# Row chunks with the high and low activations as one 512-column operand, halves added by VectorE; matrix inverse started from the identity

## The chip, the cores and the metric

The program runs on one core of one Trainium2 chip. The metric is device time in microseconds (us), the median of several executions. TensorE multiplies, VectorE (DVE) and ScalarE (ACT) read its results from PSUM, GpSimd (POOL) works on SBUF alone, SyncE (SP) issues the weight loads. PSUM has eight banks, and a bank holds 512 float32 numbers per partition.

## The reference, cut to what matters

A sequence of 256 tokens of width 1024 goes through two blocks of layers. The parts around the change:

```
u = rmsnorm(h);  proj = u @ w_in                  # a_b a_c a_v z xbc dt g_a g_b
y_a = (a_b * causal_dwconv(a_c * a_v, conv_w)) @ w_out_a          # 3 taps
xbc = silu(causal_dwconv(xbc, conv_w) + conv_b)   # 3072 channels, 4 taps
y_b = mamba2(z, xbc, dt);  h = h + (sig(g_a)*y_a + sig(g_b)*y_b) @ w_mix_out
h = h + cross_attention(rmsnorm(h), rmsnorm(mem)) # q = u @ w_q, k, v = mem @ w_kv
...
proj = h @ gdn_w_in                               # second block: 2304 channels of qkv
qkv = silu(causal_depthwise_conv(qkv, conv_w))    # 4 taps
sol = triangular_solve(I + lower, rhs)            # 64 x 64, 6 heads x 4 chunks
```

Feed-forward layers stand between these parts. Everything is float32.

## The kernel before, in words

Every weight matrix arrives as a stream of 237 chunks, each of two pieces of 128 x 1024 numbers (474 pieces). SyncE loads a piece into one of eight slots as soon as the piece eight before it is done (`piece_done`). ScalarE copies it to `w_hi`, rounded (line 1352); GpSimd makes the rest, `w_lo` = raw - `w_hi` (line 440, counted by `split_done`). Activations are split likewise, into `u_hi` and `u_lo`. A product is the sum of high x high, high x low and low x high. ScalarE calls `after(q)` in its queue, which makes `w_hi` up to six pieces ahead of piece q.

The order of all work is written out by hand, one list for each engine. A chunk's kind says how it is multiplied. In a "pair", "proj" or "acc" stage the activations are stationary and the weights move, 512 columns at a time. In a "row" stage (`row_stage`, lines 507 to 509 for its matmuls) the weights are stationary, 128 x 128, and the 256 tokens move: for each of the eight k tiles and each of two output tiles `t`, three matmuls of 256 columns into half a bank. Row chunk r uses bank r % 4 of banks 0 to 3, and waits with `row_free` for the chunk four before it. There are row stages dt, ba, mq0, mq1, kv_k and q1, and seven that the change touches, with 43 chunks: short_cv (8), short_b (4), xbc (12), mem_k (4), xq (4), mem2k (2), qkv (9).

What follows a row chunk:
- short_cv: ScalarE copies the even chunk to `ctmp`; VectorE multiplies it with the odd one (line 2171) and applies three taps (2174, 2179). short_b: VectorE multiplies (2186), ScalarE makes `h_hi` (1535), VectorE `h_lo` (2188).
- xbc and qkv (`conv` on ScalarE, `taps` on VectorE): ScalarE writes the first tap (1550, twice a chunk), VectorE adds three taps for each of two tiles from the bank (2009, six instructions), the last of which frees the bank, ScalarE applies silu (1555, counted by `conv_act`). Between the chunks VectorE runs the steps of `row_chain`, the step sizes on few rows (2025 to 2048); two of its links, an exponential and a logarithm, are ScalarE's (1572, 1574 in xbc). In xbc VectorE also scales `x_dt` (2218) behind chunks 7 to 10, after four transposes in TensorE's queue. Behind xbc, TensorE does half a z pair and then waits for all twelve `conv_act` before the scores (887). In qkv ScalarE squares each chunk (1759) and TensorE sums the squares (977) behind chunks 5, 6 and 7; behind qkv come transposes (991) and the spreads gc, kb (985).
- mem_k, xq, mem2k: one copy to SBUF (1996). mem2v, a pair stage, follows mem2k; attention follows xq.

The inverse of the 12 x 2 unit triangular 64 x 64 blocks is built by doubling: `LEVELS` 2 to 64. VectorE masks `lt` to `iE` (2494), forms I - iE (2498), TensorE transposes iE (1086), VectorE forms the transposed start (2502). Each level is then a product of 48 small matmuls (1102), a mask `iQ` (2536), twice as many products (1122, 1125), and an update `iYX` (2551). Pieces of the gz stage (`gate`) and transposes (`extra`) stand between the levels in TensorE's queue, and the scores of the memory attention in the last two (1041, with VectorE's maxima, 2510). The last level ends in `fullY` (2549), from which the products v0 (1175) are made.

## Time and profile before

| | |
|---|---|
| median of 3 runs | 1541.56 us (1540.18 to 1541.83) |
| profiled execution, whole | 1541.43 us |
| its span, first to last instruction | 1539.6 us |
| TensorE busy | 1509.3 us, 98% |
| TensorE weight loads busy | 1307.5 us, 85% |
| VectorE busy | 605.1 us, 39% |
| ScalarE busy | 830.3 us, 54% |
| GpSimd busy | 1155.9 us, 75% |
| mean granted clock of TensorE | 0.994 |

A busy share is an average over the whole span. Matmul records overlap, since each is shown from its start to the end of its results, so the time that a matmul costs is read from start to start. "idle before" names how long an engine sat idle just before an instruction, and who released it.

### The profile page before, as it was taken

The page shows a single profiled execution, that of the slowest core. Times are in us where ns is not written, and L with a number is a line of the kernel's source. Part 1 is how long each engine was busy: PE and PEld are TensorE (multiplying, and loading weights), DVE is VectorE, ACT ScalarE, POOL GpSimd, SP SyncE. Part 2 cuts the span into 40 slices and gives each one's busy share as a digit, 9 for nine tenths or more (in the row PEclk, how much of TensorE's full clock was granted, in tenths as well). Part 3 has the DMA queues.
Part 4 walks back from the last instruction along what each step waited for, and adds up shares of the span by engine and source line. Part 5 has one row for each costly group of instructions (what it writes and reads, how often), then busy time and mean ns, then how long its engine had stood idle before and what let it go on. Part 6 is the DMA issues. An engine that isn't in the chain of part 4 may idle for free.

```text
span 1539.6 us, 22902 instructions
## 1 busy us (share of the span) xinstructions
PE 1509.3 (98%) x9276; PEld 1307.5 (85%) x9276; DVE 605.1 (39%) x1008; ACT 830.3 (54%) x1293; POOL 1155.9 (75%) x499
## 2 busy tenths in 40 slices
PE   9999999999999999999999999999999999999997
PEld 7888889999878898888888898888888888888886
DVE  3111016447786712331330498772113747311101
ACT  6444364375756536364554687155445476564443
POOL 8888978888758888578869796317888963388893
PEclk9999999999999999999999999999999999999999
DMA  6555555565644555265555563105555542355552
GB/s 232 191 189 192 181 191 180 175 212 181 211 152 141 199 181 193 91 209 187 186 184 194 171 211 124 44 29 196 178 186 200 194 160 75 106 176 184 191 196 78
DMA packets 71865, 259.87 MB, mean 169 GB/s; under 512 B 7984, under 2 KB 8784, under 8 KB 71504
## 3 DMA queue, kind: packets, MB, share of 16 engines
q1 hardware_dynamic: 69552, 250.97, 49.4%
q10 hardware_dynamic: 2208, 7.43, 1.3%
q8 instruction: 74, 1.21, 0.3%
q14 instruction: 31, 0.25, 0.0%
HBM read 257.29 MB, written 1.08 MB: 168 GB/s over the span
## 4 chain that ended last, share of the span: by engine, by line
PE 83%; DVE 9%; ACT 4%; issue 2%; POOL 1%; DMA 1%; ACTq 0%; DVEq 0%; POOLq 0%
PE bank L537 14%; PE bank L539 14%; PE bank L538 13%; PE bank L567 5%; PE bank L569 5%; PE bank L568 5%; PE bank L507 5%; PE bank L509 5%; PE bank L508 5%; PE bank L681 1%; ACT w_hi L1352 1%; DVE dec L2231 1%; DVE dec L2234 1%; PE bank L653 1%; DVE sq_mem L2059 1%
## 5 line engine op out<-in xcount | busy, mean ns | idle before, releaser
L440 POOL TENSOR_TENSOR w_lo<-raw,w_hi 128x1024 fp32r<-128x1024 f32 x468 | 1129.0, 2445 | 337.6 <-ACT w_hi L1352 337.1
L1352 ACT ACTIVATE w_hi<-raw 128x1024 fp32r<-128x1024 f32 x474 | 487.9, 1058 | 286.1 <-DMA raw<-in_w 281.8
L537 PE MATMUL bank<-w_hi,u_hi 128*128 128x512 f32 x872 | 345.8, 397 | 2.4 <-POOL w_lo L464 2.0
L539 PE MATMUL bank<-w_hi,u_lo 128*128 128x512 f32 x872 | 340.9, 391 | 0.0
L538 PE MATMUL bank<-w_lo,u_hi 128*128 128x512 f32 x872 | 340.3, 390 | 0.0
L507 PE MATMUL bank<-u_hi,w_hi 128*128 128x256 f32 x688 | 196.7, 286 | 0.0
L537 PEld LDWEIGHTS bank<-w_hi,u_hi 128*128 128x128 f32 x872 | 164.3, 188 | 36.5 <-POOL w_lo L464 2.2
L509 PE MATMUL bank<-u_hi,w_lo 128*128 128x256 f32 x688 | 194.7, 283 | 0.0
L508 PE MATMUL bank<-u_lo,w_hi 128*128 128x256 f32 x688 | 194.6, 283 | 0.0
L539 PEld LDWEIGHTS bank<-w_hi,u_lo 128*128 128x128 f32 x872 | 164.0, 188 | 35.0
L538 PEld LDWEIGHTS bank<-w_lo,u_hi 128*128 128x128 f32 x872 | 164.4, 188 | 32.6
L567 PE MATMUL bank<-w_hi,h_hi 128*128 128x512 f32 x416 | 162.9, 392 | 0.0
L569 PE MATMUL bank<-w_hi,h_lo 128*128 128x512 f32 x416 | 162.0, 389 | 0.0
L568 PE MATMUL bank<-w_lo,h_hi 128*128 128x512 f32 x416 | 161.9, 389 | 0.0
L507 PEld LDWEIGHTS bank<-u_hi,w_hi 128*128 128x128 f32 x688 | 131.9, 192 | 1.6 <-issue 1.2
L508 PEld LDWEIGHTS bank<-u_lo,w_hi 128*128 128x128 f32 x688 | 132.0, 192 | 0.3
L509 PEld LDWEIGHTS bank<-u_hi,w_lo 128*128 128x128 f32 x688 | 132.0, 192 | 0.0
L1972 DVE TENSOR_TENSOR h_lo<-bank,h_hi 128x512 fp32r<-128x512 f32 x44 | 30.4, 691 | 227.9 <-ACT h_hi L1406 227.9
L1420 ACT ACTIVATE act_g<-bank,stats 128x256 f32<-128x256 f32 x88 | 41.7, 475 | 136.2 <-PE bank L539 136.1
L1985 DVE SCALAR_TENSOR_TENSOR hid<-bank,stats,act_g 128x256 f32<-128x256 f32 x88 | 42.4, 483 | 174.5 <-ACT act_g L1420 174.4
L1966 DVE SCALAR_TENSOR_TENSOR x<-bank,x 128x512 f32<-128x512 f32 x32 | 21.8, 688 | 197.2 <-PE bank L569 153.6
L569 PEld LDWEIGHTS bank<-w_hi,h_lo 128*128 128x128 f32 x416 | 78.1, 188 | 16.4
(432 smaller groups left out, 2072.0 us busy)
## 6 DMA issues: line engine op xcount, KB each, us to landing
raw<-in_w SPq DMA_DIRECT2D x474, 512.0 KB, 4.4
bc<-acs_scratch ACTq DMA_DIRECT2D x8, 512.0 KB, 4.6
mem_t<-in_mem ACTq DMA_DIRECT2D x2, 1024.0 KB, 6.3
xf<-in_x SPq DMA_DIRECT2D x2, 512.0 KB, 7.0
out<-out_t SPq DMA_DIRECT2D x4, 256.0 KB, 2.7
lvl<-in_lvl ACTq DMA_DIRECT2D x1, 448.0 KB, 3.0
band<-in_band ACTq DMA_DIRECT2D x1, 256.0 KB, 6.1
tri<-in_tri SPq DMA_DIRECT2D x1, 192.0 KB, 8.0
```

Source lines behind the costliest of these rows:

```text
L440: nc.gpsimd.tensor_tensor(w_lo[:, q % RAW, :], raw[:, q % RAW, :], w_hi[:, q % HI, :].bitcast(F32), ALU.subtract).then_inc(split_done, 1)
L507: mm(b[:, t, :], w1, hi[:, kt, :], start=first, stop=False, skip_group_check=True)
L508: mm(b[:, t, :], w1, lo[:, kt, :], start=False, stop=False, skip_group_check=True)
L509: m = mm(b[:, t, :], w0, hi[:, kt, :], start=False, stop=last, skip_group_check=True)
L537: mm(b[:], hi[:, kt, a], w_hi[:, q % HI:q % HI + 2, c], start=kt == 0, stop=False, skip_group_check=True)
L538: mm(b[:], hi[:, kt, a], w_lo[:, q % RAW:q % RAW + 2, c], start=False, stop=False, skip_group_check=True)
L539: m = mm(b[:], lo[:, kt, a], w_hi[:, q % HI:q % HI + 2, c], start=False, stop=kt == KT - 1, skip_group_check=True)
L567: mm(b, h_hi[:, q, a], w_hi[:, hsl, c], start=q == 0, stop=False)
L568: mm(b, h_hi[:, q, a], w_lo[:, rsl, c], start=False, stop=False)
L569: return mm(b, h_lo[:, q, a], w_hi[:, hsl, c], start=False, stop=q == n - 1)
L1352: fn(w_hi[:, q % HI, :], raw[:, q % RAW, :], ACT.Copy).then_inc(hi_made, 1)
L1985: v.scalar_tensor_tensor(out=hid[j % 2][:, s, :], in0=bank[FB[(2 * j + s) % 3]][:, 1, :], scalar=stat_of(norm, "rstd")[:, s:s + 1], in1=ac ...
```

## The change

The tiles of the high and low activations are interleaved (`u_both`, `mm_both`, `um_both`), so that high and low of one k tile are 512 neighbouring columns. In the seven stages `wide_stage` takes the place of `row_stage`: per k tile and output tile one matmul of 512 columns (`w_hi` against both) into a bank of its own, and one of 256 (`w_lo` against high) into its first half. A chunk then holds two of the four banks, 2r % 4 and the next. VectorE adds the two halves of each bank (`summed`, two reductions over the pair of numbers), which frees the chunk's banks (`row_free`). In mem_k, xq and mem2k the sum is written where the copy went. In short_cv, short_b, xbc and qkv it is written to one more bank (`sum_bank`), from which taps and products read; a new count `row_done` tells ScalarE, and the next sum, that its readers are through. ScalarE's copy to `ctmp` goes. Every row and pair stage waits for the last user of its bank (`freed_for`), and the second gc spread waits for the last taps of qkv, whose sum bank it uses. In the inverse, `iE`, its transposes and the first two updates go; a level 1 is added that takes the identity as its start, and the scores and maxima of memory heads 2 and 3 move behind the last level.

```diff
-LEVELS = [2, 4, 8, 16, 32, 64]
+LEVELS = [1, 2, 4, 8, 16, 32, 64]
-         ("bacols", 1), ("gc", 3), ("lcols", 1), ("kb", 3), ("masks", 1), ("la", 6), ("x0", 3)]
+         ("bacols", 1), ("gc", 3), ("lcols", 1), ("kb", 3), ("masks", 1), ("la", 6)]
...
+WIDE = ('short_cv', 'short_b', 'xbc', 'mem_k', 'xq', 'mem2k', 'qkv')
+STAGE_OF = [name for name, n, kind in ORDER if kind not in ("acc", "proj") for _ in range(n)]
...
+def banks_of(r):
+
+    name, j = STAGE_OF[r], r - G0[STAGE_OF[r]]
+    if name in WIDE:
+        return [2 * r % 4, 2 * r % 4 + 1]
+    if name.startswith("ffn"):
+        return [2 - j % 3]
+    if name in ("mq1", "q1") and r < G0["q1"] + 3:
+        return [(G0["mq1"] + (r - G0["mq1"]) % 2) % 4]
+    return [4] if (name, j) == ("gz", 2) else [r % 4]
+
+
+def freed_for(r, b):
+
+    return max([e + 1 for e in range(r) if b in banks_of(e)], default=0)
+
+
+DONE0 = {"short_b": 0, "xbc": 4, "qkv": 16}
...
-        u_hi = place("u_hi", [P, KT, S], F32R, 72)
-        u_lo = place("u_lo", [P, KT, S], F32R, 80)
+        u_both = place("u_both", [P, KT, 2, S], F32R, 72)
+        u_hi, u_lo = u_both[:, :, 0, :], u_both[:, :, 1, :]
...
+
+        def tile_bank(r, t):
+
+            return bank[banks_of(r)[t]]
+
+        def sum_bank(stage):
+
...
+
+        def memory_bank(i):
+
+            return bank[(3, 4, 3, 0)[i]]
...
+            def wide_stage(name, both, ready=None, sub=None):
+
+                j0, n = sub or (0, NUM[name])
+                for j in range(j0, j0 + n):
+                    r = G0[name] + j
+                    for h in range(2):
+                        q = P0[name] + 2 * j + h
+                        pe.wait_ge(split_done, q + 1)
+                        for t in range(2):
+                            b = tile_bank(r, t)
+                            if h == 0 and freed_for(r, banks_of(r)[t]):
+                                pe.wait_ge(row_free, freed_for(r, banks_of(r)[t]))
+                            for k in range(4):
+                                if ready and j == j0 and t == 0:
+                                    ready(4 * h + k)
+                                a, kt = slice(k * S + t * P, k * S + t * P + P), 4 * h + k
+                                mm(b[:], w_hi[:, q % HI, a], both[:, kt, :, :], start=kt == 0, stop=False, skip_group_check=True)
+                                m = mm(b[:, 0, :], w_lo[:, q % RAW, a], both[:, kt, 0, :], start=False, stop=kt == KT - 1, skip_group_check=True)
+                        m.then_inc(piece_done, 1)
-                        if h == 0 and r > 3:
-                            pe.wait_ge(row_free, r - 3)
+                        if h == 0 and freed_for(r, r % 4):
+                            pe.wait_ge(row_free, freed_for(r, r % 4))
...
-            row_stage("short_cv", u_hi, u_lo)
-            row_stage("short_b", u_hi, u_lo)
+            wide_stage("short_cv", u_both)
+            wide_stage("short_b", u_both)
...
-                row_stage("xbc", u_hi, u_lo, sub=(j, 1))
+                wide_stage("xbc", u_both, sub=(j, 1))
...
             spread("gc", 0, grow[6])
+            pe.wait_ge(W["row_done"], DONE0["qkv"] + NUM["qkv"])
             spread("gc", 1, grow[6])
...
-            for n in range(3):
-                if n == 1:
-                    gate(1, 1)
-                b = start_unit(U0["x0"] + n)
-                pe.wait_ge(W["lev_e"], 4 if n else 2)
-                for s in range(4):
-                    for p0 in (0, 64):
-                        a = slice(p0, p0 + 64)
-                        m = mm(b[a, 0, 64 * s:64 * s + 64], iE[a, 4 * n + s, :], ident[a, a], start=True, stop=True)
-                m.then_inc(unit_done, 1)
-            pe.wait_ge(row_free, G0["gz"] + 2)
...
-                    pe.wait_ge(unit_free, U0[f"inv{lev}"] + n - 2)
+                    pe.wait_ge(unit_free, U0[f"inv{lev}"] + n - 2 if li else U0["inv1"])
...
-                                m = mm(b[a, 0, o], lt[a, k % 6, c:c + 64], iX[a, k, :], start=True, stop=True)
+                                m = mm(b[a, 0, o], lt[a, k % 6, c:c + 64], iX[a, k, :] if li else ident[a, a], start=True, stop=True)
                     m.then_inc(unit_done, 1)
+                if li == 0:
+                    gate(1, 1)
+                if lev == 2:
+                    pe.wait_ge(row_free, G0["gz"] + 2)
                 for e in EXTRA_AT.get(lev, []):
                     extra(*e)
-                if li >= 4:
-                    memory_scores(2 * li - 8)
-                    memory_scores(2 * li - 7)
-                if li == 0:
-                    pe.wait_ge(W["lev_x"], 1)
+                if lev == 32:
+                    memory_scores(0)
+                    memory_scores(1)
...
-                                mm(b[a, 1, o], iY[a, k, :], iQ[a, k, :], start=True, stop=True)
+                                mm(b[a, 1, o], iY[a, k, :] if li else ident[a, a], iQ[a, k, :], start=True, stop=True)
                             for p0 in (0, 64):
                                 a = slice(p0, p0 + 64)
-                                m = mm(b[a, 0, o], iQ[a, k, :], iY[a, k, :], start=True, stop=True)
+                                m = mm(b[a, 0, o], iQ[a, k, :], iY[a, k, :] if li else ident[a, a], start=True, stop=True)
                     m.then_inc(W["s_step"], 1)
+            memory_scores(2)
+            memory_scores(3)
...
-                act.wait_ge(piece_done, a + 2)
-                if j >= 2:
-                    act.wait_ge(row_free, g - 2)
-                fn(ctmp[j % 2][:], bank[g % 4][:], ACT.Copy).then_inc(W["short_act"], 1)
...
-                    act.wait_ge(piece_done, done(stage, j + 1))
+                    act.wait_ge(row_free, G0[stage] + j + 1)
...
-                        m = fn(dst[:, i, :], bank[g % 4][:, t, :], ACT.Identity, scale=col(wname, k * i + k - 1), **kw)
+                        m = fn(dst[:, i, :], sum_bank(stage)[:, t, :], ACT.Identity, scale=col(wname, k * i + k - 1), **kw)
...
-                    act.wait_ge(row_free, G0[stage] + j + 1)
+                    act.wait_ge(W["row_done"], DONE0[stage] + j + 1)
...
+            def summed(stage, j, out):
+
+                for t in range(2):
+                    m = v.tensor_reduce(out[:, t, :], tile_bank(G0[stage] + j, t)[:].rearrange("p a c -> p c a"), AX.X, ALU.add)
+                m.then_inc(row_free, 1)
+
+            def sum_rows(stage, dst, j0=0, n=None):
+
+                for j in range(j0, n if n is not None else NUM[stage]):
+                    dve.wait_ge(piece_done, done(stage, j + 1))
+                    summed(stage, j, dst(j))
+
...
+                    dve.wait_ge(piece_done, done(stage, j + 1))
+                    if j:
+                        dve.wait_ge(W["row_done"], DONE0[stage] + j)
+                    summed(stage, j, sum_bank(stage))
                     dve.wait_ge(W["conv_first"], (0 if stage == "xbc" else 12) + j + 1)
-                    b = bank[(G0[stage] + j) % 4]
+                    b = sum_bank(stage)
                     for d in range(1, k):
                             if d == k - 1 and t == 1:
-                                m.then_inc(row_free, 1)
+                                m.then_inc(W["row_done"], 1)
...
+                dve.wait_ge(piece_done, P0["short_cv"] + 4 * j + 2)
+                summed("short_cv", 2 * j, ctmp[j % 2])
                 dve.wait_ge(piece_done, P0["short_cv"] + 4 * j + 4)
+                summed("short_cv", 2 * j + 1, sum_bank("short_cv"))
+                dve.wait_ge(row_free, g + 2)
+                v.tensor_tensor(cv[:, 2 * j:2 * j + 2, :], ctmp[j % 2][:], sum_bank("short_cv")[:], ALU.mult).then_inc(W["short_act"], 1)
                 dve.wait_ge(W["short_act"], j + 1)
-                v.tensor_tensor(cv[:, 2 * j:2 * j + 2, :], ctmp[j % 2][:], bank[(g + 1) % 4][:], ALU.mult).then_inc(row_free, 2)
-                dve.wait_ge(row_free, g + 2)
...
-                v.tensor_tensor(cc[:, a, :], cc[:, a, :], bank[(G0["short_b"] + j) % 4][:], ALU.mult).then_inc(row_free, 1)
+                summed("short_b", j, sum_bank("short_b"))
+                dve.wait_ge(row_free, G0["short_b"] + j + 1)
+                v.tensor_tensor(cc[:, a, :], cc[:, a, :], sum_bank("short_b")[:], ALU.mult).then_inc(W["row_done"], 1)
...
-            copy_rows("mem_k", lambda j: k_t[:, 2 * j:2 * j + 2, :], 0, 1)
+            sum_rows("mem_k", lambda j: k_t[:, 2 * j:2 * j + 2, :], 0, 1)
             merged_lo(2)
             merged_lo(3)
-            copy_rows("mem_k", lambda j: k_t[:, 2 * j:2 * j + 2, :], 1)
+            sum_rows("mem_k", lambda j: k_t[:, 2 * j:2 * j + 2, :], 1)
...
-            copy_rows("xq", lambda j: q_t[:, 2 * j:2 * j + 2, :])
+            sum_rows("xq", lambda j: q_t[:, 2 * j:2 * j + 2, :])
...
-            copy_rows("mem2k", lambda j: mk[j][:])
+            sum_rows("mem2k", lambda j: mk[j][:])
...
-            for c in range(2):
-                for p0 in (0, 64):
-                    a = slice(p0, p0 + 64)
-                    v.tensor_tensor(iE[a, 6 * c:6 * c + 6, :], lt[a, :, 256 * c + p0:256 * c + p0 + 64],
-                                    lvl[a, 0:1, a].to_broadcast([64, 6, 64]), ALU.mult).then_inc(W["lev_e"], 1)
-            dve.wait_ge(W["lev_e"], 4)
-            dve.wait_ge(W["eye_set"], 1)
-            v.tensor_tensor(iY, eye[:].unsqueeze(1).to_broadcast([P, GS, 64]), iE[:], ALU.subtract).then_inc(W["lev_x"], 1)
-            for n in range(3):
-                u = U0["x0"] + n
-                dve.wait_ge(unit_done, u + 1)
-                v.tensor_tensor(iX[:, 4 * n:4 * n + 4, :], eye[:].unsqueeze(1).to_broadcast([P, 4, 64]),
-                                bank_of(u)[:, 0, :].rearrange("p (k c) -> p k c", c=64), ALU.subtract).then_inc(unit_free, 1)
-            v.memset(fullY[64:P, :, 0:64], 0.0).then_inc(W["full_zero"], 1)
-
...
+                if li == 0:
+                    v.memset(fullY[64:P, :, 0:64], 0.0).then_inc(W["full_zero"], 1)
+                    dve.wait_ge(W["eye_set"], 1)
...
-                if li >= 4:
-                    memory_max(2 * li - 8)
-                    memory_max(2 * li - 7)
+                if lev == 32:
+                    memory_max(0)
+                    memory_max(1)
...
                     else:
-                        v.tensor_tensor(iYX[:, :, a, :], iYX[:, :, a, :], b, ALU.subtract).then_inc(unit_free, 1)
+                        now = iYX[:, :, a, :] if li else eye[:].unsqueeze(1).unsqueeze(1).to_broadcast([P, 2, 4, 64])
+                        v.tensor_tensor(iYX[:, :, a, :], now, b, ALU.subtract).then_inc(unit_free, 1)
+            memory_max(2)
+            memory_max(3)
```

## Rows read from the trace of the kernel before

**Rows 1.** The page, part 1: busy time, share of the span, instructions, by engine.
```profile
PE 1509.3 (98%) x9276; PEld 1307.5 (85%) x9276; DVE 605.1 (39%) x1008; ACT 830.3 (54%) x1293; POOL 1155.9 (75%) x499
```

**Rows 2.** Timeline of TensorE in short_cv: start, length, instruction.
```profile
240.11 0.28 PE L507 MATMUL bank<-u_hi,w_hi 128*128 128x256 f32 x1
...
241.55 0.28 PE L507 MATMUL bank<-u_hi,w_hi 128*128 128x256 f32 x1
```

**Rows 3.** Timeline of TensorE in mem2v, a pair stage.
```profile
870.53 0.39 PE L538 MATMUL bank<-w_lo,um_hi 128*128 128x512 f32 x1
...
875.54 0.39 PE L539 MATMUL bank<-w_hi,um_lo 128*128 128x512 f32 x1
```

**Rows 4.** Groups by form, VectorE: busy, mean ns of one, idle before.
```profile
L2091 DVE TENSOR_REDUCE small<-bank 128x2 f32<-128x512 f32 x4 | 2.8, 691 | 3.3 <-PE bank L735 3.1
```

**Rows 5.** Busy time in stretches: PE, PEld, DVE, ACT, POOL; granted clock; DMA.
```profile
319.00:393.00 74.00, 73.45 (x613) 73.08 (x612) 48.52 (x88) 48.50 (x67) 61.38 (x26) 1.00 0.60 199
...
886.00:942.00 56.00, 54.84 (x453) 52.55 (x453) 52.50 (x74) 45.64 (x62) 49.49 (x21) 1.00 0.56 187
...
977.00:1013.00 36.00, 34.99 (x822) 33.15 (x821) 25.12 (x57) 10.74 (x33) 0.00 (x0) 0.93 0.01 4
```

**Rows 6.** Timeline of VectorE, dt and xbc.
```profile
318.61 0.47 DVE L2198 TENSOR_SCALAR rows<-bank,par 32x256 f32<-32x256 f32 x1 [2.19 <-PE bank L509]
...
347.51 2.40 DVE L2035 TENSOR_TENSOR rows<-rows,rows 32x256 f32<-32x256 f32 x1
...
352.50 2.51 DVE L2039 TENSOR_TENSOR rows<-rows,rows 32x256 f32<-32x256 f32 x1
...
373.55 2.69 DVE L2009 SCALAR_TENSOR_TENSOR xbc<-bank,par,xbc 128x255 f32<-128x255 f32 x6 [2.68 <-ACT xbc L1550]
```

**Rows 7.** Timeline of ScalarE, xbc.
```profile
333.11 1.28 ACT L1572 ACT_TABLE_LOAD   x1
334.41 0.42 ACT L1572 ACTIVATE rows<-rows 32x256 f32<-32x256 f32 x1
...
336.62 0.99 ACT L1550 ACTIVATE xbc<-bank,par 128x256 f32<-128x256 f32 x2
```

**Rows 8.** Timeline of TensorE, end of the first z half.
```profile
397.63 0.59 PE L887 MATMUL bank<-xbc 128*128 128x256 f32 x2
```

**Rows 9.** Timeline of VectorE from mem2k to qkv.
```profile
872.18 1.27 DVE L1996 COPY mk<-bank 128x512 f32<-128x512 f32 x2
...
886.66 0.42 DVE L2400 COPY grow<-bank 6x256 f32<-6x256 f32 x1
...
889.60 4.74 DVE L2411 COPY pick<-ident 6x768 f32<-6x768 f32 x2
...
915.35 0.40 DVE L2035 TENSOR_TENSOR grow<-grow,grow 6x256 f32<-6x256 f32 x1
```

**Rows 10.** Timeline of TensorE, the first two gc spreads behind qkv.
```profile
942.47 2.00 PE L985 MATMUL bank<-grow,pick 128*128 128x256 f32 x8
```

**Rows 11.** Timeline of VectorE, short_cv.
```profile
240.94 8.00 DVE L2179 SCALAR_TENSOR_TENSOR cc<-cv,par,cc 128x255 f32<-128x255 f32 x4
...
253.81 1.79 DVE L2179 SCALAR_TENSOR_TENSOR cc<-cv,par,cc 128x255 f32<-128x255 f32 x4
```

**Rows 12.** Timeline of VectorE, last copy of xq.
```profile
629.11 0.69 DVE L1996 COPY q_t<-bank 128x512 f32<-128x512 f32 x1 [5.06 <-PE bank L509]
```

**Rows 13.** Timeline of VectorE, the inverse and its end.
```profile
964.01 9.31 DVE L2494 TENSOR_TENSOR iE<-lt,lvl 64x384 f32<-64x384 f32 x4
...
1010.33 0.69 DVE L2510 TENSOR_REDUCE small<-bank 128x2 f32<-128x512 f32 x1 [1.83 <-PE bank L1041]
```

**Rows 14.** Timeline of TensorE, the inverse.
```profile
968.24 0.68 PE L1086 MATMUL bank<-ident,iE 64*64 64x64 f32 x16
...
976.82 2.83 PE L1102 MATMUL bank<-iYX,lt 64*64 64x64 f32 x48 [2.20 <-DVE iYX L2502]
...
985.68 1.64 PE L1102 MATMUL bank<-iYX,lt 64*64 64x64 f32 x48
```

60 lines of the change are left out of this document (29 added, 31 removed).

## The prediction

> **What bounds the kernel now.** I read the page's busy shares first, then the waits and the timelines of the seven converted stages. TensorE is busy 98% of the span [rows 1], so only two things can shorten the run: fewer or shorter TensorE starts, or the 30 us in which it is idle (1539.6 - 1509.3). Every other engine costs nothing so long as it stays hidden. In the two convolution stages that cover is thin. Over xbc VectorE is busy 48.5 of 74 us, and over qkv 52.5 of 56 us; the granted clock is full in both [rows 5]. So VectorE in qkv has 3.5 us to spare, and the change gives it 18 more instructions there. That is the pair of numbers to keep in mind.
>
> **TensorE's saving.** A unit of a row stage (one k tile, one output tile) is three matmuls of 256 columns. From the first to the last row there are 12 starts in 1.44 us, 0.120 us each [rows 2], so 0.360 us a unit. The unit becomes one matmul of 512 columns and one of 256. In a pair stage 22 starts of 512 columns take 5.01 us, 0.228 us each [rows 3]. So a unit becomes 0.228 + 0.120 = 0.348 us, a chunk of 16 units 5.57 instead of 5.76 us: 0.19 us a chunk, 8.2 us over 43 chunks if nothing else stirred. The columns are the same 768; only one start's overhead of some 13 ns goes. Bounds of the unit: 0.360 (no gain) and 0.320 (768 columns at 2.4 GHz, no overhead at all; 27 us over all chunks). I take 0.348, which both rows give directly. The Trainium skill (TensorE: Matmul & The Clock Gate, Back-to-back issue gap) gives N/2.4 + 2.5 ns as the gap between starts; by that rule one start less would save 2.5 ns a unit, 1.7 us in all, an estimate from that page. The rows show 13 ns a start, and the measurement decides.
>
> **VectorE's new work.** Each chunk gets two reductions, each reading 512 numbers from PSUM. A reduction of 512 elements from PSUM takes 0.69 us [rows 4]; two back to back overlap a little, as the two copies that took 1.27 us [rows 9]. I take 1.3 us a chunk. That row reads neighbours and writes two numbers, whereas here the two summands lie 1 KB apart and 256 numbers are written, which no row shows. Upper bound 2.4 us a pair (the 512-element operations blocked by GpSimd are the nearest slow ones), lower bound 0.6 us (one pass over 512). The Trainium skill (VectorE: DVE Perf Modes, Rules for kernel authors) speaks against this part of the change: it calls the reduction the slowest VectorE operation, fixed at single rate, and advises restructuring where it is on a hot path.
>
> The order matters more than the length. Before, ScalarE's first tap of chunk j ran beside VectorE's taps of chunk j-1, and four banks let TensorE run up to four chunks ahead. Now the sum of chunk j waits for the taps of j-1 (one shared sum bank), ScalarE's first tap waits for the sum, VectorE's taps wait for ScalarE, and a chunk holds two banks, so TensorE can start chunk j only when the sum of j-2 is done. A turn of VectorE is then 1.3 (sums) + 1.0 (ScalarE, VectorE idle) [rows 7] + 2.7 (six taps) [rows 6] + 0.1 of handshakes = 5.1 us, before the small row steps between the chunks; TensorE needs 5.57.
>
> **xbc, walked.** Origin is the end of dt (318.6, where VectorE's bias row starts [rows 6]). Row steps by the trace: three steps after chunk 3 take 7.4 us (first and last of three [rows 6]), about 2.3 us after chunk 0, 0.3 after chunk 1, 3.6 after chunk 2, 1.8 after chunk 4; the steps of chunks 1 and 2 wait for a table load and an exponential or logarithm [rows 7]. x_dt adds 1.3 after chunks 7 to 10.
>
> | chunk | TensorE starts | sum done | taps done | VectorE free |
> |---|---|---|---|---|
> | 0 | 0.0 | 6.9 | 10.6 | 13.0 |
> | 2 | 11.1 | 20.5 | 24.6 | 29.2 |
> | 3 | 16.7 | 30.5 | 34.2 | 41.6 |
> | 4 | 22.3 | 42.9 | 46.7 | 48.4 |
> | 5 | 30.5 (2.7 late) | 49.7 | 53.5 | 53.5 |
> | 6 | 43.0 (6.9 late) | 54.8 | 58.5 | 58.8 |
> | 7 | 49.7 (1.0 late) | 60.1 | 63.8 | 65.1 |
> | 11 | 75.5 | 85.4 | 89.1 | 89.1 |
>
> TensorE is through xbc and the first z half at 88.1, but behind it waits for all twelve silus, at 89.8. The same walk of the kernel before gives 79.0, and the trace has 397.63 - 318.6 = 79.0 [rows 8]: the walk holds. Cost +10.8 us. With the pair at 2.4 us the walk gives 102.6 (+23.6), with 0.6 us 83.1 (+4.1). VectorE enters the decay chain 12 us later and TensorE the z pieces 10.8 us later, so at most 1.2 us could be added there; I take none. The load queue is no part of it: SyncE issues each raw piece when a piece is done, so it waits along with TensorE, and the DMA engines are 60% busy [rows 5]; ScalarE's and GpSimd's splits run ahead of TensorE and run dry instead of late. ScalarE also loses its four copies of short_cv, which saves nothing. The first xbc chunk also needs dt's bank back (0.47 us [rows 6]): +0.5.
>
> **qkv, walked the same way.** ba's bank is needed by chunk 0 (free at 887.1 [rows 9]), and VectorE is busy with the pick copies until 894.3 [rows 9]. Sums are done at 895.6, 902.8, 908.9, 919.7, 930.0, 938.7, 947.4, 952.2 and 961.1. TensorE is held 4.8 us before chunk 5, then 6.8, 3.8 and 1.7 us by the square sums, which wait for ScalarE's squares, which in its queue now stand behind a first tap that waits for a sum. Taps end at 964.6. (The same walk of before has TensorE through qkv at 942.2; the trace starts the gc spreads, behind two short transposes, at 942.47 [rows 10].) The second gc spread uses the sum bank and waits for the last taps; it stood in the middle of the row that starts at 942.47 [rows 10], at 943.3. Cost +21.3 us, +30 with the pair at 2.4, +16.5 at 0.6.
>
> **Other borders.** short_out needs the bank of the last short_b sum: +1.35. short_cv's first chunk needs gate_a's last sigmoid: +0.65. xq's first needs mem_v's last copy, +0.7, and attention waits for a pair of reductions in place of one copy of 0.69 [rows 12]: +0.6. mem2v, which started at 870.2, needs mem2k's sum, which VectorE reaches at 872.2 [rows 9], so 873.5: +3.3. In short_cv one set of four taps took 8.0 us where the others took 1.8 [rows 11]; with two banks a chunk such a set holds TensorE up to 4 us: I take 2, between 0 and 4. The 20 chunks outside xbc, qkv and mem2k save 3.8.
>
> **The inverse.** Gone are the masking of 9.3 us [rows 13] and the 3 us behind it. But gate pieces lay beside them: the last wait for VectorE there is 2.2 us [rows 14]. Now: the products of level 1 behind gate(1,0) at 968.3 [rows 14], 1.6 us as the 48 rows at 985.68 [rows 14], gate(1,1) 2.9, the second products (twice as many, same pace) 3.0: level 2 at 975.8 instead of 976.8, and its first part takes 1.6 instead of 2.8 us [rows 14]: -2.2. At the end, two maxima no longer stand before fullY [rows 13]: -1.8. Sum -4.
>
> **Sum.** -3.8 + 10.8 + 0.5 + 21.3 + 6.6 + 2.0 - 4.0 = +33.4 us. Against it stands a relief: while TensorE stalls GpSimd runs dry, and then row steps are short. One and the same step took 2.40 us in xbc and 0.40 in qkv [rows 6, 9], with GpSimd busy 83% and 88% of the two stretches [rows 5]. The walk has some 24 us of such excess; GpSimd's share falls by a tenth in xbc and by a quarter in qkv, worth about 4 us. The result is +29.5 on the profiled execution's 1541.4 us (span 1539.6 and 1.8 around it, 0.1 below the median of the runs): **1571 us**.
>
> **The rivals.**
> *All of it hidden (faster).* If the row steps took 0.4 us throughout and a pair 0.6 us, the walks give -3.0 in xbc and +3 in qkv; with borders of 5.0 (short_cv's stall gone), the inverse at -4 and the saving of 3.8, that is -2.8; a unit of 0.320 would take up to 19 more off: 1520 to 1539. It decides only if VectorE's pair falls below about 0.6 us and GpSimd stops blocking. For it: the stalls themselves relieve GpSimd. Against: six taps and ScalarE's first tap alone fill 3.7 us of each turn. Chance 0.07, and 0.05 for no change.
> *Relief larger than taken.* Row steps of 0.4 us with a pair of 1.3 us: +1.6 and +7.5, in all about +8.5: 1550. Chance 0.10.
> *Reductions at half rate for the 1 KB stride.* +23.6, +30, borders 4 more: +60, 1601 us. Nothing in the trace bears on it. Chance 0.12.
> *The clock.* Where TensorE waits in the inverse the granted clock is 0.93 over 36 us [rows 5], 2.5 us lost. Stalls of 7 us may do the same in xbc and qkv: +2 to +5, inside the forecast.
> *The forecast* (1558 to 1590) has 0.66.
>
> **Range and chances.** 1552 to 1600 leaves out the faster and equal cases, the lowest relief and the worst of the half rate. 0.2% (3 us) is about what a measurement here can tell. Faster 0.07, same 0.05, slower 0.88.
>
> **What would show it.** Starts of 0.228 and 0.120 us in turn; reductions near 0.69 us, one ending before each first tap; TensorE waiting for VectorE's sums in xbc (3, 7 us) and qkv, and for squares there; a wait before the second gc spread; level 2 of the inverse at most 1 us earlier relative to the last lt. The forecast is wrong if VectorE's row steps shorten to 0.4 us throughout, or if the reductions are not near 0.69 us.

## The result, and the profile after

The changed kernel takes 1582.44 us (median of 4 runs, 1580.27 to 1583.85), the kernel before 1541.43 (1540.18 to 1541.83): a ratio of 1.0269, 95% interval 1.0257 to 1.0281, 41.0 us slower. The page of the profiled execution (span 1582.0 us) answers to [rows 1]:

```profile
PE 1520.5 (96%) x8688; PEld 1280.6 (81%) x8688; DVE 629.8 (40%) x1082; ACT 829.4 (52%) x1289; POOL 1156.9 (73%) x499
```

TensorE is idle for 61.5 us (1582.0 - 1520.5) where it was idle for 30.3. VectorE has 24.7 us more to do on balance: the reductions take 55 us, while copies, the masking of the inverse and waits for GpSimd inside other instructions are gone. That is little for an engine busy 40% of the span; what it costs depends on where it stands. The view of waits of TensorE names the places (waiting line, releaser, us in total, times, longest):

```profile
PE bank L561 <- DVE bank L2038: 11.1, 4, 4.8
PE bank L561 <- DVE ctmp L2038: 8.2, 2, 7.2
PE bank L1030 <- ACT l2sq L1802: 5.3, 1, 5.3
PE bank L1038 <- DVE qkv L2068: 4.9, 1, 4.9
...
PE bank L590 <- DVE mk L2038: 3.1, 1, 3.1
...
PE bank L880 <- DVE x_dt L2282: 2.0, 1, 2.0
```

L561 is the first matmul of `wide_stage` and L2038 the reduction: 19.3 us of waits for sums. L1030 are the square sums, L1038 the gc spreads, L880 the transposes behind xbc chunks. Following one start of TensorE through both timelines gives the loss by stage. "Later by" is how much later than before the named work starts:

| start of | before, us | after, us | later by | added by the stage ahead of it |
|---|---|---|---|---|
| short_cv | 224.64 | 224.88 | 0.2 | 0.2 |
| short_out | 293.75 | 304.73 | 11.0 | 10.7 |
| dt | 315.54 | 326.59 | 11.1 | 0.1 |
| scores behind xbc | 397.63 | 421.40 | 23.8 | 12.7 |
| mem2k | 857.22 | 880.56 | 23.3 | -0.4 |
| ba, behind mem2v | 882.70 | 910.39 | 27.7 | 4.4 |
| kb products, behind qkv and the spreads | 958.47 | 1005.35 | 46.9 | 19.2 |
| v products, behind the inverse | 1017.10 | 1059.33 | 42.2 | -4.6 |

The reductions are what the prediction took them for. The groups by form of VectorE answer to [rows 4]; 58 of them take 0.685 us each, and a pair stands in the timelines as 1.28 to 1.30 us:

```profile
L2038 DVE TENSOR_REDUCE bank<-bank 128x256 f32<-128x512 f32 x58 | 37.2, 685 | 26.0 <-PE bank L562 25.9
...
L2038 DVE TENSOR_REDUCE k_t<-bank 128x256 f32<-128x512 f32 x8 | 5.2, 686 | 16.7 <-PE bank L562 16.7
```

**short_cv.** VectorE's timeline answers to [rows 11]. The two scalings and four taps of the first pair took 5.0 + 10.0 us, and the sums that give banks back stand behind them:

```profile
238.42 5.01 DVE L2236 TENSOR_SCALAR cc<-cv,par 128x256 f32<-128x256 f32 x2
243.47 10.00 DVE L2241 SCALAR_TENSOR_TENSOR cc<-cv,par,cc 128x255 f32<-128x255 f32 x4
253.40 1.28 DVE L2038 TENSOR_REDUCE ctmp<-bank 128x256 f32<-128x512 f32 x2
```

In the kernel before, the two scalings ahead of the set of 8.0 us took 3.7:

```profile
237.24 3.67 DVE L2174 TENSOR_SCALAR cc<-cv,par 128x256 f32<-128x256 f32 x2
```

TensorE's timeline at the same place:

```profile
247.36 0.28 PE L562 MATMUL bank<-u_both,w_lo 128*128 128x256 f32 x1
254.82 0.76 PE L561 MATMUL bank<-u_both,w_hi 128*128 128x512 f32 x1 [7.18 <-DVE ctmp L2038]
255.38 0.41 PE L562 MATMUL bank<-u_both,w_lo 128*128 128x256 f32 x1
255.59 0.63 PE L561 MATMUL bank<-u_both,w_hi 128*128 128x512 f32 x1
...
258.80 0.41 PE L561 MATMUL bank<-u_both,w_hi 128*128 128x512 f32 x1
259.05 0.28 PE L562 MATMUL bank<-u_both,w_lo 128*128 128x256 f32 x1
```

And the view of stretches for the 7.2 us behind the wait (length, busy time of PE, PEld, DVE, ACT and POOL, then the granted clock):

```profile
254.80:262.00 7.20, 7.18 (x31) 6.20 (x32) 4.14 (x9) 0.00 (x0) 0.88 (x1) 0.72 0.15 46
```

TensorE waited 7.18 us. Behind it 12 starts took 3.98 us (254.82 to 258.80), where 12 take 2.12 at full clock: 1.9 us more, at the 1.2 GHz level, called half clock below. The reader is to see that a wait has a second price, and that it is paid in busy time: the records of 0.63 us are matmuls that take 0.40 elsewhere.

**xbc and qkv.** The same pattern, in TensorE's timeline: one wait in xbc, then the three long ones of qkv and the spreads behind it:

```profile
370.17 0.76 PE L561 MATMUL bank<-u_both,w_hi 128*128 128x512 f32 x1 [4.50 <-DVE bank L2038]
...
946.44 0.76 PE L561 MATMUL bank<-u_both,w_hi 128*128 128x512 f32 x1 [4.76 <-DVE bank L2038]
...
966.86 1.92 PE L1030 MATMUL bank<-l2sq,ones_at 128*32 128x256 f32 x8 [5.34 <-ACT l2sq L1802]
...
989.23 2.06 PE L1038 MATMUL bank<-grow,pick 128*128 128x256 f32 x4 [4.90 <-DVE qkv L2068]
```

The stretches of xbc and of qkv with the spreads answer to [rows 5], where the clock was full in both; now it is 0.95 and 0.91. (The wait before the second gc spread ends where the second stretch does, so the starts at half clock behind it are not in it.)

```profile
326.60:421.40 94.80, 84.68 (x470) 72.81 (x468) 68.24 (x121) 52.61 (x72) 64.58 (x27) 0.95 0.51 167
...
910.40:989.20 78.80, 63.83 (x343) 52.11 (x341) 61.31 (x103) 48.86 (x67) 50.54 (x21) 0.91 0.47 153
```

The row steps of qkv got shorter. VectorE's instructions on grow and lrow took 26.0 us before and 18.6 now; those of xbc on 32 x 256 rows took 15.8 and 15.7. Two of the steps behind chunk 3 of qkv, before and after; GpSimd subtracted beside them before, and was idle (947.3 to 950.8) after:

```profile
915.78 2.52 DVE L2037 SCALAR_TENSOR_TENSOR grow<-grow,grow 6x256 f32<-6x256 f32 x1
918.33 2.52 DVE L2039 TENSOR_TENSOR grow<-grow,grow 6x256 f32<-6x256 f32 x1
```
```profile
950.24 0.41 DVE L2096 SCALAR_TENSOR_TENSOR grow<-grow,grow 6x256 f32<-6x256 f32 x1
950.68 0.41 DVE L2098 TENSOR_TENSOR grow<-grow,grow 6x256 f32<-6x256 f32 x1
```

**The inverse.** TensorE's timeline answers to [rows 14]: the products of level 1 with the identity, their second half behind gate(1,1), and level 2, which no longer waits:

```profile
1015.12 1.61 PE L1145 MATMUL bank<-ident,lt 64*64 64x64 f32 x48
...
1019.74 0.33 PE L1167 MATMUL bank<-iQ,ident 64*64 64x64 f32 x4
...
1022.59 1.64 PE L1145 MATMUL bank<-iYX,lt 64*64 64x64 f32 x48
```

The 4.65 us that the inverse gives back come in three parts, read from the starts of the same work: level 2 starts 1.1 us earlier, the 5.3 us of work from there on take 2.3 us less, since they no longer run at half clock behind waits of 1.5 and 2.2 us, and 1.2 come at the end, before v0. So half of it is clock.

### The profile page after: what moved, and what is told of

It is laid out like the page before. It is cut to its first block, busy times and chain, and to the rows that moved or that the text cites. A ratio compares the mean times of both kernels' runs of the same rounds, so it can differ in the third digit from the quotient of the medians.

```text
span 1582.0 us, 21804 instructions
## 1 busy us (share of the span) xinstructions
PE 1520.5 (96%) x8688; PEld 1280.6 (81%) x8688; DVE 629.8 (40%) x1082; ACT 829.4 (52%) x1289; POOL 1156.9 (73%) x499
## 4 chain that ended last, share of the span: by engine, by line
PE 78%; DVE 12%; ACT 5%; issue 3%; POOL 1%; DMA 1%; ACTq 0%; DVEq 0%; POOLq 0%
PE bank L590 13%; PE bank L592 13%; PE bank L591 13%; PE bank L622 5%; PE bank L620 5%; PE bank L621 5%; PE bank L561 5%; PE bank L562 2%; DVE bank L2038 1%; PE bank L734 1%; DVE xbc L2068 1%; ACT w_hi L1399 1%; DVE cc L2241 1%; PE bank L540 1%; PE bank L542 1%
## 5 line engine op out<-in xcount | busy, mean ns | idle before, releaser
L590 PE MATMUL bank<-w_hi,u_both 128*128 128x512 f32 x872 | 346.3, 397 | 2.4 <-POOL w_lo L497 2.0
L592 PE MATMUL bank<-w_hi,u_both 128*128 128x512 f32 x872 | 340.8, 391 | 0.0
L591 PE MATMUL bank<-w_lo,u_both 128*128 128x512 f32 x872 | 340.5, 390 | 0.0
L561 PE MATMUL bank<-u_both,w_hi 128*128 128x512 f32 x592 | 219.2, 412 | 20.8 <-DVE bank L2038 11.1
L590 PEld LDWEIGHTS bank<-w_hi,u_both 128*128 128x128 f32 x872 | 164.2, 188 | 36.5 <-POOL w_lo L497 2.2
L592 PEld LDWEIGHTS bank<-w_hi,u_both 128*128 128x128 f32 x872 | 164.2, 188 | 35.3
L591 PEld LDWEIGHTS bank<-w_lo,u_both 128*128 128x128 f32 x872 | 164.5, 189 | 32.7
L562 PE MATMUL bank<-u_both,w_lo 128*128 128x256 f32 x592 | 169.7, 287 | 0.0
L561 PEld LDWEIGHTS bank<-u_both,w_hi 128*128 128x128 f32 x592 | 116.0, 196 | 52.8 <-issue 24.3
L562 PEld LDWEIGHTS bank<-u_both,w_lo 128*128 128x128 f32 x592 | 116.3, 196 | 0.0
L621 PEld LDWEIGHTS bank<-w_lo,h_hi 128*128 128x128 f32 x416 | 78.1, 188 | 16.0
L620 PEld LDWEIGHTS bank<-w_hi,h_hi 128*128 128x128 f32 x416 | 78.1, 188 | 15.9
```

Of the source, the lines that this page charges most:

```text
L561: mm(b[:], w_hi[:, q % HI, a], both[:, kt, :, :], start=kt == 0, stop=False, skip_group_check=True)
L562: m = mm(b[:, 0, :], w_lo[:, q % RAW, a], both[:, kt, 0, :], start=False, stop=kt == KT - 1, skip_group_check=True)
L590: mm(b[:], hi[:, kt, a], w_hi[:, q % HI:q % HI + 2, c], start=kt == 0, stop=False, skip_group_check=True)
L591: mm(b[:], hi[:, kt, a], w_lo[:, q % RAW:q % RAW + 2, c], start=False, stop=False, skip_group_check=True)
L592: m = mm(b[:], lo[:, kt, a], w_hi[:, q % HI:q % HI + 2, c], start=False, stop=kt == KT - 1, skip_group_check=True)
L620: mm(b, h_hi[:, q, a], w_hi[:, hsl, c], start=q == 0, stop=False)
```

## The experiments

All times are medians beside those of the kernel before on the same chip (1540.34 us for the first four, 1540.27 for the next four, 1540.02 for the last four), and the ratios are taken to these; the forecasts started from the 1541.4 and 1582.4 us of the first chip, so 1 us between them and a median decides nothing. Losses "in the trace" are read like the table above. The diffs are cut to the lines that matter; guards for stages that are not wide are left out.

**New inverse alone.** `WIDE` is empty, so all 43 chunks are as before.

```diff
-WIDE = ('short_cv', 'short_b', 'xbc', 'mem_k', 'xq', 'mem2k', 'qkv')
+WIDE = ()
```


> The kernel before with the new inverse alone (no wide stage). In the changed kernel the inverse gave back 4.6 us between the gate piece that starts at 962.3 before (1009.2 after, 46.9 later) and v0 (42.2 later). Theory: this is a gain of its own, so 1541.4 - 4.6 = 1536.8 us. Rival: the gain is only what a late VectorE left over behind qkv (the gate pieces found their banks free for once), then it is gone here: 1541 us, within 1 us of before.

Measured 1536.92 us, ratio 0.9979 (0.9970 to 0.9988), so 3.4 us less than the kernel before on this chip, between 1.8 and 4.6. In the trace the stretch from the kb products to the v products is 4.65 us shorter, as in the changed kernel. The gain is its own and the rival falls. That the number itself was hit is partly luck: the forecast started from 1541.4, and the kernel before takes 1540.3 here. It is the only part of the change whose gain a median shows.

**xbc and qkv back on rows.**

```diff
+WIDE = ('short_cv', 'short_b', 'mem_k', 'xq', 'mem2k')
```


> The changed kernel with xbc and qkv back on three matmuls of 256 columns and four banks; the other five stages stay wide. TensorE lost 12.8 us in xbc and 18.9 us in qkv. Theory (these losses are made inside the two stages, by the turn of VectorE): 1582.4 - 31.7 = 1550.7 us. Rival (part of it is carried in from short_cv, where VectorE ends 11 us late, or is clock lost for good): less comes back, 1558 us or more.

Measured 1556.41 us, 1.0102 (1.0087 to 1.0117). In the trace the two stages lose 0.0 and 0.1 us, so the 12.7 and 19.2 us are made inside them. Of the 5.7 us by which the total missed, 2.9 are in short_cv and short_b, which lost 13.6 us here in place of 10.7: the taps of the third pair took 8.1 us in place of 6.0, TensorE's second wait was 3.3 us in place of 1.0, and it had starts at half clock behind it. Another 0.8 are longer half clock behind the same wait before mem2v. The code of these stages is the same in both kernels; one tap more was held up.

**The sums first.** Chunk j + 1 is summed ahead of the taps of chunk j.

```diff
 for j in range(n):
-    sum_up(j)
+    if j == 0 or j >= PRESUM[stage]: sum_up(j)      # PRESUM: xbc 7, qkv 9
+    if j + 1 < PRESUM[stage]: sum_up(j + 1)         # two sum banks by turns
     taps of chunk j
```


> All seven stages stay wide and VectorE does the same instructions, but it sums chunk j + 1 ahead of the taps of chunk j, in two sum banks by turns (xbc: the first seven chunks; qkv: all nine), and in short_cv the first sum of the next pair ahead of the four taps. Theory (the order costs, not the length of the sums): the banks come back 2.7 us or a row step earlier and ScalarE's first tap lies beside taps again; short_cv loses 2 to 4 us in place of 10.7, xbc 1 to 4 in place of 12.8, qkv 4 to 8 in place of 18.9: 1550 us, between 1546 and 1556. Rival (VectorE has too much work, whatever its order: 1.3 us a chunk more on 21 chunks is 27 us): no more than 10 us come back, 1572 us or more.

Measured 1570.24 us, 1.0198 (1.0179 to 1.0216): 12 us back, not 32. The waits of TensorE say where the rest stayed:

```profile
PE bank L564 <- DVE bank L2042: 6.3, 1, 6.3
PE bank L892 <- DVE rows L2118: 4.9, 1, 4.9
```

No chunk of xbc waits for a bank any more (its loss is 5.9 us in place of 12.7, qkv's 11.5 in place of 19.2), so the order, with the second sum bank that it needs, was worth 14.5 us in these two. In qkv 6.7 us are waited at the first two gc spreads, whose banks are now both sum banks, and 2.9 for squares. But the row steps now come a chunk later, and the transposes of the step sizes (L892) wait 4.9 us for them: a wait that I had not listed. In short_cv moving one chunk's sum of the pair gave 1.2 us (9.5 lost in place of 10.7); 6.3 us are waited for the other's.

**One reduction a chunk in xbc and qkv.**

```diff
-for t in range(2):
+for t in ((1,) if stage in ("xbc", "qkv") else (0, 1)):
     m = v.tensor_reduce(...)
```


> The changed kernel with one reduction a chunk in place of two in xbc and qkv (the sum of the first output tile is left out, what reads it reads old numbers), so a pair of 1.3 us is one of 0.69. Theory: my walk with a pair of 0.6 us gives 6.7 us less in xbc and 4.8 less in qkv, 11.5 us: 1571 us. Rival (the work of the sums is the whole cost of the two stages, 31.7 us): half of it goes, 1566 us or less. Rival (the sums cost nothing by their length, only by the place where they stand): within 4 us of 1582.

Measured 1570.62 us, 1.0199 (1.0182 to 1.0216), as the walk with a pair of 0.6 us gave; 6.2 us came back in xbc and 6.8 in qkv. A turn that is 0.6 us shorter, 21 times, gives 13 us, and both rivals fall. It is not a price for each us of sums, though, as the kernel without sums below shows.

**The product in PSUM.** Only the place of one tile changes, with the reads of it and one wait that protects it.

```diff
-v.tensor_tensor(cv[:, 2*j:2*j+2, :], ctmp[j % 2][:], sum_bank("short_cv")[:], ALU.mult)
+v.tensor_tensor(sum_bank("short_cv")[:], ctmp[j % 2][:], sum_bank("short_cv")[:], ALU.mult)
```


> The changed kernel; in short_cv the product of the two sums stays in the sum bank (PSUM) instead of going to cv in SBUF, and the two scalings and four taps of a pair read it there. Same instructions, same order. Theory (these instructions have SBUF operands alone and are held up by GpSimd's subtractions of 2.4 us each, while the taps of xbc, which read PSUM, take 0.45 us each beside the same GpSimd): the 5.0 + 10.0 us of the first pair become 0.6 + 1.8, TensorE's wait of 7.2 us in short_cv and its 1.9 us at half clock go, and 9 to 10 us come back: 1573 us. Rival (the output and the second operand are in SBUF still, so they are held up as before): within 2 us of 1582.

Measured 1571.86 us, 1.0199 (1.0174 to 1.0225). VectorE's timeline has for the same six instructions:

```profile
236.78 0.88 DVE L2238 TENSOR_SCALAR cc<-bank,par 128x256 f32<-128x256 f32 x2
237.69 1.78 DVE L2243 SCALAR_TENSOR_TENSOR cc<-bank,par,cc 128x255 f32<-128x255 f32 x4
```

0.9 + 1.8 us in place of 5.0 + 10.0, while GpSimd made 19 subtractions in a row (208.3 to 253.4) beside them. TensorE does not wait once in short_cv, and short_cv with short_b loses 0.3 us. The Trainium skill (SBUF — State Buffer, Who interferes with whom) has the rule: a VectorE instruction with two SBUF inputs, or in a two-port mode, shares an exclusive pair of ports with GpSimd, one with at most one SBUF input outside those modes does not. The taps, with two SBUF inputs before and one now, agree with it on both sides, at 2.5 us an instruction against 0.45. The scalings have one SBUF input, so by the rule they can be held up only in a two-port mode. Two of them took 5.0 us beside GpSimd, 0.6 with GpSimd idle and 0.9 from PSUM, which fits such a mode but does not show it.

**short_cv back on rows.** The taps stay in SBUF, but behind four banks.

```diff
+WIDE = ('short_b', 'xbc', 'mem_k', 'xq', 'mem2k', 'qkv')
```


> The changed kernel with short_cv alone back on three matmuls of 256 columns, four banks and ScalarE's copies; its taps are as they were, with SBUF operands. Theory (with four banks a chunk a set of taps of 12 us is hidden, as it was before): short_cv and short_b lose 1 to 1.5 us in place of 10.7: 1573 us. Rival (part of the loss comes from short_b or from GpSimd, which runs ahead more): no better than 1576.

Measured 1574.86 us, 1.0214 (1.0187 to 1.0240), 1.9 us above the forecast but not outside what single runs vary (1572.12 to 1575.76); the rival's 1576 is as near, so the trace has to decide. In the trace short_cv and short_b lose 2.3 us, 0.9 and 1.4 of it waits; xbc loses 11.2 here in place of 12.7. Slow taps lose little with four banks and 8 us more with two.

**Sums first, product in PSUM, cols behind chunk 7.**

```diff
# on top of the edits of "The sums first" and "The product in PSUM"
-if j == 6:
+if j == 7:
     b = start_unit(U0["cols"])
```


> The kernel with the sums first, and with it the product in PSUM and the transposes of the step sizes (cols) behind chunk 7 of xbc in place of chunk 6. In the kernel with the sums first TensorE lost 9.5 us in short_cv and short_b and waited 4.9 us for the row steps at these transposes. Theory (two waits of their own, each with its cause named): 1570.2 - 8.5 - 4.9 = 1557 us, between 1553 and 1560. Rival (the stalls relieve each other: with short_cv mended GpSimd is busier in xbc and the row steps and square sums take the time back): 1562 us or more.

Measured 1558.34 us, 1.0112 (1.0082 to 1.0142). The number was right, one reason was not. short_cv gave its 9.2 us, but moving the transposes gave 0.7 (xbc loses 5.2 in place of 5.9): behind them the transposes of `xbc` waited 4.0 us for a silu instead, since the second sum bank is one of theirs and has to be free. It is the best form of the wide convolutions that was found, and 21 us slower than none at all.

**Six banks for short_cv.**

```diff
+if name == "short_cv":
+    return [(0, 1), (2, 3), (5, 6)][j % 3]
```


> The changed kernel with six banks instead of four for the chunks of short_cv (0 and 1, 2 and 3, 5 and 6 by turns), VectorE's work and order as they are. Theory (two banks a chunk leave TensorE two chunks ahead; a set of 15 us on VectorE then shows): with three chunks TensorE meets it 5.6 us later, the wait of 7.2 us shrinks to 1 to 2, the half clock behind it and the second wait of 1.0 go: about 8 us back, 1574 us. Rival (the depth is not what limits, VectorE only falls further behind and the wait comes at a later chunk): 1579 us or more.

Measured 1579.71 us, 1.0250 (1.0220 to 1.0280). TensorE waits once, for 3.4 us, and loses 1.5 more at half clock behind it. VectorE's timeline has two slow sets of taps in place of one, and below it GpSimd's, where they begin:

```profile
241.38 10.12 DVE L2243 SCALAR_TENSOR_TENSOR cc<-cv,par,cc 128x255 f32<-128x255 f32 x4
...
258.73 8.00 DVE L2243 SCALAR_TENSOR_TENSOR cc<-cv,par,cc 128x255 f32<-128x255 f32 x4
```

```profile
219.85 41.09 POOL L475 TENSOR_TENSOR w_lo<-raw,w_hi 128x1024 fp32r<-128x1024 f32 x17
```

With TensorE running on, GpSimd subtracted until 260.9, where it stopped at 255.7 in the changed kernel, and held up the next set too. In the trace the loss is 5.8 us in place of 10.7. The medians show less of it, 2.7 us, with single runs between 1576.95 and 1583.72. The time is the rival's; of the mechanism each had half: depth hides the first set, and takes away the pause that made the second one fast.

**No sums in xbc and qkv.**

```diff
-summed(stage, j, sum_bank(stage))
-b = sum_bank(stage)
+b = tile_bank(G0[stage] + j, t)      # its first half; the last tap frees both banks
```


> The changed kernel without any reduction in xbc and qkv: the first tap and the taps read the first half of each tile's bank, as the last tap frees both banks (the product of high weights with low activations is left out of these two stages; TensorE still makes it). TensorE's instructions, the two banks a chunk and the bank order stay. Theory (the sums, by their length and by their place in the chain, cost all of the 12.7 + 18.9 us; two banks a chunk alone cost nothing, since the longest turn of VectorE, 2.7 us of taps and 7.4 of row steps, is shorter than two chunks): all of it comes back and 1 us a stage is saved, 1549 us, between 1547 and 1553. Rival (two banks a chunk in place of one is itself what lets the row steps through to TensorE): 1555 us or more.

Measured 1558.65 us, 1.0117 (1.0099 to 1.0134), 10 us above my number. For qkv the theory holds: 1.0 us lost in place of 19.2. (With the sum bank the wait of 4.9 us before the second gc spread goes too.) For xbc it falls: 7.5 us are lost without a single sum. TensorE's timeline shows the waits, now for the last tap:

```profile
358.99 0.47 PE L561 MATMUL bank<-u_both,w_hi 128*128 128x512 f32 x1 [1.01 <-DVE xbc L2062]
...
368.94 0.77 PE L561 MATMUL bank<-u_both,w_hi 128*128 128x512 f32 x1 [4.07 <-DVE xbc L2062]
```

So in xbc two banks a chunk alone let the row steps through. I had compared the longest turn (10.1 us) with two chunks (11.2) and left out that the turns before it had eaten the lead. It is also 1.0 us more than xbc loses with one sum a chunk (6.5): without sums the three row steps behind chunk 3 take 7.4 us, as in the kernel before, and with one or two sums 5.4, since they meet GpSimd at another moment. Less work on VectorE was not less time here.

**Two row step tiles in PSUM.**

```diff
+rows[1], rows[4] = bank[6][:, 0, :], bank[7][:, 0, :]
```


> The changed kernel with two of the row step tiles of xbc (the ones that most steps read or write) in free PSUM banks, so that nine of the twelve steps have at least one operand there. Same instructions and order. Theory (these steps wait for GpSimd's subtractions: their excess over 0.4 us, and 0.28 for one input, adds to 9 us in xbc, and it falls in the turns behind which TensorE waits): TensorE loses 3 to 5 us in xbc in place of 12.7, 1574 us, between 1571 and 1577. Rival (the chain of sum, first tap and taps holds TensorE whatever the steps take): within 3 us of 1582.

Measured 1572.85 us, 1.0221 (1.0205 to 1.0236). xbc loses 3.9 us in place of 12.7, and the rival falls. (Another 2 us came back in short_cv, which the edit does not touch; see below.) The row steps take 8.8 us in place of 15.7. The steps of L2096 and L2098 in the changed kernel, and the same two here (L2097, L2099), each with two inputs, both in SBUF there and one here:

```profile
363.77 2.57 DVE L2096 SCALAR_TENSOR_TENSOR rows<-rows,rows 32x256 f32<-32x256 f32 x1
366.38 2.44 DVE L2098 TENSOR_TENSOR rows<-rows,rows 32x256 f32<-32x256 f32 x1
```
```profile
359.07 0.42 DVE L2097 SCALAR_TENSOR_TENSOR bank<-bank,rows 32x256 f32<-32x256 f32 x1
359.52 0.41 DVE L2099 TENSOR_TENSOR rows<-rows,bank 32x256 f32<-32x256 f32 x1
```

The last two results belong together. Without sums xbc loses 7.5 us, with sums but short row steps 3.9, with both 12.7. So the sums are worth 5.2 us and the waits of the row steps for GpSimd 8.8, by themselves nearly the whole, and neither is "the" cause. Both runs keep two banks a chunk; no run has these with neither sums nor slow row steps.

**What pays, put together.** mem_k alone wide, with the new inverse; then short_cv and short_b as well, product in PSUM.

```diff
+WIDE = ('mem_k',)
+WIDE = ('short_cv', 'short_b', 'mem_k')      # the second kernel
```


> The kernel before with the new inverse and with mem_k alone wide. mem_k was 0.7 us shorter in the changed kernel and nothing behind it waited longer. Theory: 1536.9 - 0.7 = 1536.2 us, faster than both kernels. Rival (the 0.7 us are lost to the next wait): 1537 us, the same as the new inverse alone.

> As the kernel with mem_k alone wide, and with short_cv and short_b wide as well, the product in PSUM. TensorE's saving of 0.10 us a chunk there (1.2 us over 12) stands against a first chunk that waits for gate_a's last sigmoid and a wait of 1.4 us before short_out. Theory: 0.4 to 0.7 us slower than with mem_k alone, 1536.7 us. Rival (the two waits were there before in other places): 1.2 us faster than it, 1535.0 us.

Measured 1536.47 us, 0.9976 (0.9966 to 0.9986), and 1536.63 us, 0.9981 (0.9972 to 0.9990). Both beat the kernel before; mem_k is 0.7 us shorter in both traces, but the three kernels with the new inverse can't be told apart by time (1536.9, 1536.5, 1536.6), so neither theory nor rival is decided by it. In the trace of the second kernel short_cv and short_b lose 0.3 us, the wait of 1.4 before short_out in it, which is the theory's side. Where nothing waits the wide form is worth next to nothing.

## Why the prediction was right, and where it was short

The sign, the range and the two large places were right. The likeliest number, 1571, was 11 us short. By its own steps:

- **The unit** (0.348 us): 0.347 in xq, 0.350 in mem_k and 0.353 in short_cv, worked out from the starts. mem_k gave its 0.7 us of 23.9. Over short_cv and short_b that is 1.2 us in place of 2.3. Right in size; the saving is small because the same 768 columns are multiplied and one start in three goes.
- **VectorE's pair** (1.3 us): right. The 1 KB stride costs nothing. The Trainium skill's advice (VectorE: DVE Perf Modes, Rules for kernel authors) against reductions on a hot path proved sound for its place in the chain, not for its rate: a reduction of 512 took as long as a copy of 512.
- **xbc** (+11.3 with the border): 12.7, of which 3.8 us are starts at half clock, so the waits cost 2.4 us less than walked. The walk had waits of 2.7, 6.9 and 1.0 us; TensorE waited 1.0, 4.5 and 0.9 for sums, 0.7 for the row steps, and 2.0 for `x_dt`, which the walk did not have. The row steps were no shorter in all (15.7 us against 15.8), but those behind chunk 3 took 5.4 in place of 7.4, and those behind chunk 4 took 4.9 in place of 1.7.
- **qkv** (+21.3): 19.2. Waits of 4.8 and 5.3 us came where the walk put 4.8 and 6.8, and 4.9 at the second gc spread. Starts at half clock took 6.4 us of it (2.4 + 2.4 + 1.6 behind the three), so by waits alone the walk was 8.5 us too long. The row steps explain 7.4 of it (26.0 us before, 18.6 now; four ran in 0.3 to 0.4 us that had taken 2.1 to 2.5, and others still took over 2). The relief was thus larger than the 4 us taken: 10.9 by this account (2.4 in xbc, 8.5 in qkv).
- **mem2v** (+3.3): 4.4, a wait of 3.1 and 1.6 at half clock, less the saving. **The other borders**: short_out waited 1.4 us (1.35 foreseen) for the last reduction, which ended at 304.63; xq and attention lost 0.8 net of the saving (0.5 foreseen).
- **short_cv's stall** (+2): 10.1 us, the step that failed: waits of 7.2 and 1.0 us and 1.9 at half clock. The mechanism stood in the prediction, with a bound of 4 us from the set of 8.0; I took the middle, although the trace of before, with its scalings of 3.7 us, gives 15.0 us from one sum to the next (1.3 + 0.7 + 3.7 + 8.0 + 1.3) against 11.2 of TensorE's, that is 3.8. The set then took 10.0 us and its scalings 5.0, so even the bound was too low. GpSimd's subtractions ran without a break beside them, where before they had one of 0.6 us inside the set.
- **The clock** (2 to 5 us, "inside the forecast"): about 13.7 us in all (1.9 + 3.8 + 1.6 + 6.4), and it was in no term of the sum. In xbc and qkv it cost 10.2 us and the relief beyond the 4 taken gave 6.9 back. That these two came out at 31.9 us, where 28.6 were foreseen (11.3 + 21.3 - 4), is two errors of opposite sign, and luck.
- **The inverse** (-4): -4.65. Level 2 starts 1.1 us earlier (1.0 foreseen), its first part takes 1.64 us in place of 2.83 (1.2 foreseen), the work behind it another 1.1 less (not foreseen), and the end gives 1.2 (1.8 foreseen). The granted clock over the inverse rose from 0.94 to 1.00: the 2.3 us of the second and third part are half clock that is gone, of which the sum had the first 1.2 without calling it that.

Of the rivals, "all of it hidden" needed short pairs and short row steps together. The pairs stayed at 1.3, and the kernel without sums, but with slow row steps, still loses 7.5 us in xbc. The half rate did not happen. In sum, on the span: short_cv and its border 9.0 above the forecast (its 1.9 of half clock in it), half clock elsewhere 11.8, and the other way the relief 6.9 and the rest 1.1. That is 12.8 above the 29.5 foreseen, where the spans differ by 42.4 us (1582.0 - 1539.6), 12.9 above.

The same short_cv code waits 5.1 to 5.2 us at its first wait with one reduction a chunk and with row steps in PSUM, and 7.2 in the changed kernel, with xbc and qkv back on rows and without sums. The set of taps takes 10.0 us in all of them; the difference lies in the two scalings ahead of it, 5.0 us in the changed kernel and 2.95 with one reduction a chunk:

```profile
238.32 2.95 DVE L2238 TENSOR_SCALAR cc<-cv,par 128x256 f32<-128x256 f32 x2
```

So one scaling was held up for one subtraction of GpSimd's, or was not. What decides it stays open: how the two engines meet was not controlled in any run but the one that moved the product.

## What to carry to other kernels

Before an operation is moved onto an engine that is mostly idle, walk the turn that the new work joins (who waits for whom, and how many turns the buffers cover), and bound it by the slowest set of instructions that the trace shows at that place, with what stands ahead of it, not by their mean: here 25 us of work (net) on an engine busy 39% cost 47 us (42.4 and the 4.6 that the inverse gave). When a buffer scheme is halved, ask which slow turns it has been hiding. A stall of TensorE is to be priced with the matmuls at half clock behind it, and an instruction of VectorE whose operands all lie in SBUF with GpSimd's instruction beside it; one operand moved to PSUM was worth 10 us here.

## What the runs showed of the hardware

In the changed kernel each of the seven waits of TensorE between 2.0 and 7.2 us in the changed stages had starts at 1.2 GHz behind it, and these cost 1.5 to 2.4 us more. At four of them, of 4.5 us and more, the granted clock had fallen during the wait (in the one of 7.2 us, 2.8 us before work came back); at the other three it fell as work came back or up to 0.5 us later, and 0.8 us later behind the wait of 3.4 us in the kernel with six banks.

The length of a wait did not fix its price. The same wait of 3.1 us before mem2v, in ten kernels, was followed by between 2.9 and 5.9 us at half clock, 1.4 to 3.0 us lost. Waits of 2.0 us for `x_dt` (row steps in PSUM, six banks) and one of 2.9 for squares (sums first with the product in PSUM) were followed by none, while the same ones in other kernels were. The waits of 1.0 us in short_cv and xbc were followed by none, but in the kernel with the new inverse alone two waits of 1.0 us, 2.3 us apart (at 1240.9 and 1243.2), were. Such an episode costs 1 to 2 us, and it comes and goes between traces in stages that no edit touches: near 19 us into the kernel before it is there, and in the kernel with the new inverse alone it is not.

A VectorE tap with both inputs in SBUF took up to 2.5 us beside GpSimd's subtractions of 2.4 us each, and 0.45 us with one input in PSUM, in the same place of the program. A reduction that adds 2 x 256 float32 numbers from PSUM, the summands 1 KB apart, took 0.685 us, as long as a copy of 512 (0.69).
